# A hybrid decoder layer: zeros on TensorE at the start, 128 keys for the first query block, and a later place for the query lows

## What is computed

```python
h = h + 0.5 * swiglu(rmsnorm(h, ffn1_norm), ffn1_w_gate, ffn1_w_up, ffn1_w_down)   # 1024 -> 2816 -> 1024
proj = rmsnorm(h, mix_norm) @ w_in             # xp (512), q (16 heads of 64), k, v (2 heads), gates (2 x 1024)
branch_pool = causal_pool_mixer(xp, pool_w, pool_scale) @ w_pool_out
branch_attn = sliding_window_sink_attention(q, k, v, q_norm, k_norm, sinks) @ w_attn_out
h = h + (sigmoid(gate_pool) * branch_pool + sigmoid(gate_attn) * branch_attn) @ w_out
h = h + 0.5 * swiglu(rmsnorm(h, ffn2_norm), ffn2_w_gate, ffn2_w_up, ffn2_w_down)

# attention: nb = 4 blocks of 128 queries; each sees its own block of keys and the one before
kk = jnp.concatenate([jnp.pad(kb, pad)[:, :-1], kb], axis=2)      # block 0: 128 keys of zero padding
scores = einsum(qb, kk) * HEAD_DIM ** -0.5
band = (rel >= 0) & (rel < WINDOW)             # WINDOW = 128
in_seq = (nb > 0) | (kj >= 0)                  # block 0 sees none of the padding
scores = where(band & in_seq, scores, float32 min)
probs = softmax(concatenate([scores, sink]))[..., :-1]
out = einsum(probs, vv)
```

## Time and profile before

| | us |
|---|---|
| three runs of the kernel | 1060.41, 1062.83, 1062.62; median 1062.62 |
| the profiled execution, its own time | 1062.52 |
| its span, first to last instruction | 1060.7 |
| PE busy in it | 1044.2 |
| DVE, ACT, POOL busy | 663.9, 471.5, 433.6 |
| mean granted clock of PE | 0.998 |

### The profile page before, as it was taken

How to read it: one execution, slowest core, us unless ns; L and a number is a source line. 1 busy time by engine, 2 the same in 40 slices (tenths; PEclk the granted TensorE clock), 3 DMA queues, 4 the chain that set the end, 5 groups by cost and what they waited for, 6 DMA issues and landing times.

```text
span 1060.7 us, 15343 instructions
## 1 busy us (share of the span) xinstructions
PE 1044.2 (98%) x5952; PEld 907.8 (86%) x5952; DVE 663.9 (63%) x996; ACT 471.5 (44%) x814; POOL 433.6 (41%) x238
## 2 busy tenths in 40 slices
PE   7999999999999999999999999999999999999998
PEld 6878999998888888887777788888899999988887
DVE  6898777659340278426767657669997677584101
ACT  6443554455231334246667643333444555563120
POOL 1543423425444453345445445434423423354441
PEclk9999999999999999999999999999999999999999
DMA  5724757713323432221111122306367667333332
GB/s 194 226 81 122 186 152 182 204 62 119 100 99 93 146 112 80 88 89 60 60 60 59 60 61 99 99 27 201 99 159 181 188 168 188 104 100 99 99 99 99
DMA packets 42144, 124.76 MB, mean 118 GB/s; under 512 B 4320, under 2 KB 5344, under 8 KB 42080
## 3 DMA queue, kind: packets, MB, share of 16 engines
q1 hardware_dynamic: 37616, 107.89, 30.8%
q0 software_dynamic: 4320, 15.73, 8.6%
q10 hardware_dynamic: 144, 0.26, 0.1%
HBM read 121.76 MB, written 2.10 MB: 117 GB/s over the span
## 4 chain that ended last, share of the span: by engine, by line
PE 89%; DVE 7%; issue 1%; ACT 1%; DMA 1%; POOL 0%; DVEq 0%; SPq 0%; ACTq 0%
PE psum L524 18%; PE psum L526 18%; PE psum L525 18%; PE psum L619 10%; PE psum L620 9%; PE psum L621 9%; PE psum L854 1%; PE psum L869 1%; DVE u_blocks L1560 1%; PE psum L882 1%; PE psum L884 1%; PE psum L883 1%; DVE moving_sums_low L1585 1%; DMA up_s<-weights_dram 1%; PE psum L763 1%
## 5 line engine op out<-in xcount | busy, mean ns | idle before, releaser
L1394 POOL TENSOR_TENSOR w_low_in_place<-w_raw,w_high 128x1024 fp32r<-128x1024 f32 x68 | 169.6, 2497 | 212.3 <-ACT w_high L948 212.1
L948 ACT ACTIVATE w_high<-w_raw 128x1024 fp32r<-128x1024 f32 x118 | 124.5, 1055 | 212.9 <-DMA w_raw<-weights_dram 172.3
L1394 POOL TENSOR_TENSOR w_low<-w_raw,w_high 128x1024 fp32r<-128x1024 f32 x50 | 121.6, 2434 | 111.1 <-ACT w_high L948 111.1
L524 PE MATMUL psum<-hidden_high,w_high 128*128 128x512 f32 x352 | 137.0, 389 | 0.0
L525 PE MATMUL psum<-hidden_low,w_high 128*128 128x512 f32 x352 | 137.0, 389 | 0.0
L526 PE MATMUL psum<-hidden_high,w_low_in_place 128*128 128x512 f32 x352 | 136.9, 389 | 0.0
L1509 DVE SCALAR_TENSOR_TENSOR h<-psum,h 128x512 f32<-128x512 f32 x24 | 16.5, 689 | 151.0 <-PE psum L526 151.0
L524 PE MATMUL psum<-u_high,w_high 128*128 128x512 f32 x240 | 98.2, 409 | 0.0
L526 PE MATMUL psum<-u_high,w_low 128*128 128x512 f32 x240 | 93.9, 391 | 0.0
L525 PE MATMUL psum<-u_low,w_high 128*128 128x512 f32 x240 | 93.8, 391 | 0.0
L524 PE MATMUL psum<-ffn_u_high,w_high 128*128 128x512 f32 x222 | 88.6, 399 | 2.0 <-POOL w_low_in_place L1394 2.0
(11 more groups left out here) (259 smaller groups left out, 2849.6 us busy)
## 6 DMA issues: line engine op xcount, KB each, us to landing
w_raw<-weights_dram SPq DMA_DIRECT2D x118, 512.0 KB, 3.5
gate_a<-weights_dram SPq DMA_DIRECT2D x15, 512.0 KB, 6.1
gate_s<-weights_dram SPq DMA_DIRECT2D x15, 512.0 KB, 3.6
gate_s<-weights_dram POOLq DMA_DIRECT2D x15, 512.0 KB, 7.1
up_a<-weights_dram SPq DMA_DIRECT2D x15, 512.0 KB, 4.7
up_s<-weights_dram SPq DMA_DIRECT2D x15, 512.0 KB, 3.6
up_s<-weights_dram POOLq DMA_DIRECT2D x15, 512.0 KB, 8.3
gate_a<-weights_dram SPq DMA_DIRECT2D x15, 256.0 KB, 5.8
```

The lines of the kernel that those rows point to most:

```text
L524: pe.matmul(o, wh, xh, start=start, stop=False)
L948: act.activation(high[:, s, :], raw[:, s, :], ACT.Copy).then_inc(high_done, 1)
L1394: pool.tensor_tensor(wlow[:, s, :], raw[:, s, :], high[:, s, :], ALU.subtract).then_inc(low_done, 1)
```

## The change

Three parts.

1. **Zeros on PE at the start.** `first_tile` begins with `spin`: as soon as `sum_of_squares` is cleared, PE multiplies it with itself, five plain float32 products of 256 columns into a bank that is written afresh later. DVE waits for them (`spun`) before it adds the first square.

The diff, cut to its core:

```diff
@@
+        def is_first(nb):
+            return isinstance(nb, int) and nb == 0
+        def keys(nb):
+            return slice(BLK, 2 * BLK) if is_first(nb) else slice(0, 2 * BLK)
+        def halves(nb):
+            return (1,) if is_first(nb) else (0, 1)
+        def turned_count(nb, j):
+            return j if is_first(nb) else 8 * nb - 4 + 2 * j
@@ PE
+            def spin():
+                pe.wait_ge(summed[0], 1)
+                for i in range(5):
+                    mm = pe.matmul(psum[:, 0, 0:HT], acc[:, 0:P], acc[:, 0:HT], start=True, stop=True)
+                mm.then_inc(spun, 1)
@@ PE first_tile
+                spin()
                 pe.wait_ge(u_high[0], 1)
                 pe.wait_ge(quarter_high, 1)
@@ PE scores
-                            mm = pe.matmul(psum[:, 4 + kv, hh * 2 * BLK:(hh + 1) * 2 * BLK],
-                                           qs[r, 2 * j + hh, :], ks[r, :], start=(n == 0), stop=(n == 2))
+                            o = psum[:, 4 + kv, hh * 2 * BLK + keys(nb).start:(hh + 1) * 2 * BLK]
+                            mm = pe.matmul(o, qs[r, 2 * j + hh, :], ks[r, keys(nb)], start=(n == 0), stop=(n == 2))
@@ PE turn, weigh
-                for k in range(2):
+                for k in halves(nb):
...
-                pe.wait_ge(pt_low, 8 * nb + 2 * j + 2)
+                pe.wait_ge(pt_low, turned_count(nb, j) + len(halves(nb)))
@@ PE (and the same on ACT and DVE; POOL: all of block 0, then the loop from 1)
-            with pe.Fori(0, NB - 1) as nb:
+            for j in range(1, SLOTS):
+                step(0, j)
+            step(1, 0)
+            with pe.Fori(1, NB - 1) as nb:
@@ ACT exps
-                    act.activation(prob[:, j % 2, a, :], prob[:, j % 2, a, :], ACT.Exp,
+                    p = prob[:, j % 2, a, keys(nb)]
+                    act.activation(p, p, ACT.Exp,
@@ POOL normalize
-                p = prob[:, j % 2, :, :]
-                pool.tensor_tensor(p, p, rden[:, j % 2, :].unsqueeze(2).to_broadcast([P, 4, 2 * BLK]),
+                p = prob[:, j % 2, :, keys(nb)]
+                width = 2 * BLK - keys(nb).start
+                pool.tensor_tensor(p, p, rden[:, j % 2, :].unsqueeze(2).to_broadcast([P, 4, width]),
@@ DVE start
             second_half(1)
+            dve.wait_ge(spun, 1)
             for c in range(DT):
                 add_square(0, c, c)
@@ DVE
-            dve.memset(kn[:, 0:BLK], 0.0).then_inc(k_ready, 1)
-            dve.memset(vtok[:, 0, :], 0.0).then_inc(v_ready, 1)
@@ DVE maxima
-                dve.wait_ge(mask_set, nb + 1)
...
-                    dve.tensor_tensor_reduce(prob[:, b, a, :], psum[:, 4 + kv, hh * 2 * BLK:(hh + 1) * 2 * BLK],
-                                             mask[:, :], 1.0, 4 * MASKED, ALU.add, ALU.max,
+                    o = psum[:, 4 + kv, hh * 2 * BLK + keys(nb).start:(hh + 1) * 2 * BLK]
+                    dve.tensor_tensor_reduce(prob[:, b, a, keys(nb)], o,
+                                             consts[:, C_MASK + keys(nb).start:C_MASK + 2 * BLK],
+                                             1.0, 4 * MASKED, ALU.add, ALU.max,
@@ DVE step
-                    dve.tensor_copy(mask[:, :], consts[:, C_MASK:C_MASK + 2 * BLK]).then_inc(mask_set, 1)
                     block_factors(nb)
                 maxima(nb, j)
+                turned_part(*before)
+                if j in (1, 2):
+                    pool_gate(nb, j - 1)
                 if j == SLOTS - 1 and not (isinstance(nb, int) and nb == NB - 1):
                     stage(nb + 1)
-                if j in (1, 2):
-                    pool_gate(nb, j - 1)
-                turned_part(*before)
                 denominators(nb, j)
```

More of the change, by code:

```diff
@@ L1465, in _ @@
                 low_part(U_GATE + s, s)
-            step(0, 0)
-            with pool.Fori(0, NB - 1) as nb:
+            for j in range(SLOTS):
+                step(0, j)
+            step(1, 0)
+            with pool.Fori(1, NB - 1) as nb:
                 for j in range(1, SLOTS):
```

56 lines of the change are left out of this document (37 added, 19 removed).

## The result

| | before | after |
|---|---|---|
| time, median (range) | 1062.19 us (1060.41 to 1062.83) | 1050.67 us (1049.52 to 1052.04) |
| ratio to before, 95% interval | 1 | 0.9895 [0.9877, 0.9912] |
| profiled execution: time, span | 1062.52, 1060.7 | 1052.04, 1050.1 |

The change makes the kernel 1.05% faster, 11.5 us by the medians and 10.5 by the two profiled executions.

What follows compares the result with a forecast made beforehand. PE, busy 1044.2 of 1060.7 us, was taken to bound the kernel. From 1062.52, minus 1.6 (start), minus 6.3 (block 0), plus 2.4 (narrow scores), minus 2.3 (order) gave 1054.7 us, range 1051.1 to 1058.4.

Steps and rivals of the forecast that it cites:

- the price of the narrow scores: Block 0's score products on 128 columns: plain-f32 rate assumed, 0.22 us a pair, adding 2.4 us over four steps.
- cheap end: Block 0's narrow scores: a pair costs as one transpose of 128 columns, 0.11 us, changing the total by -0.2 us.
- Start, -1.6: Kernel start: zeros raise PE's clock early, the 25th product starts at 12.44, and 1.6 us are saved.
- The bounds of -0.3 and -2.6 for single runs: Kernel start: the gain from zeros varies between these values in single runs, as the moment of the clock's rise differs.
- Block 0, -6.3 without the scores' price: Attention, block 0 on 128 keys: four steps fall from 37.43 to 31.1 us, 1.9 of it waits.
- Order, -2.3: Attention, query lows behind probability lows: steps 3 of blocks 1 and 2 save 1.4 us, steps 1 save 0.9.
- The fall of the clock, kept: First FFN, 72.7 to 76.1 us: PE's clock still falls, costing some 1.6 us; its going only widens the range.
- (a): Block 0's scores: narrow score products are cheap, giving 1052.1 us; chance 0.32.
- (b): Block 0: other engines hold steps at 8.89 us, so only the waits go, giving 1056.7 us; chance 0.08.
- (e): Block 0's scores: a narrow pair costs 0.87 us instead of 0.15, making the kernel slower at 1069.3 us; chance 0.04.
- (c): Start: zeros don't count as work for the clock, or the DVE chain eats the gain, 1056.3 us; chance 0.07.
- (d): Block changes: query lows come late under POOL's low part, adding 4.2 us at three changes, 1058.9 us; chance 0.04.

Runs made afterwards that it cites:

- e4: Changed kernel with block 0's scores taken over 256 columns again instead of 128; 1051.6 us.
- e11: Changed kernel with block 0's scores taken over only the last 64 of its 128 keys; 1050.4 us.
- e2: Kernel before with only block 0 cut to its own 128 keys, no zeros and the old VectorE order; 1054.75 us, ratio 0.9928.
- e16: One more profile of the e2 kernel, unchanged and without zeros; 1052.93 us.
- e5: Changed kernel with VectorE's copy of the next block's key factors split and taken out of the head of step 0; 1049.61 us, ratio 0.9879.
- e1: Kernel before with only the five products of zeros at the start and VectorE's wait for them; 1060.32 us, ratio 0.9978.
- e3: Kernel before with only VectorE's order changed: probability lows first, then pool gate, then next block's query lows; 1060.76 us, ratio 0.9979.

## Why the prediction was wrong

**The failed step is the price of the narrow scores**, "So I take the dear end: +2.4". This term of the sum was mis-sized, and its mechanism was wrong. It is not +2.4 but -0.6: four times the 0.15 us between e4 and the changed kernel. The argument was that the two narrow kinds in the trace ran at 0.85 ns a column, as plain float32 does, and the fast rate was shown for wide products only. But the transposes' 0.11 us for 128 columns is not a rate a column; e11 shows 0.11 for 64 columns too. So the price of a narrow pair has a floor that doesn't follow its columns. The transposes and the narrow scores have in common that 128 columns of new weights are loaded each time, and that load is the likely floor. The row for the right answer was in hand, the transposes as the "cheap end", and that rival had 0.32.

The rest, term by term (profile against profile):

- **Start, -1.6:** measured -1.54, of which 0.36 came only in the first FFN. The 25th product is at 12.88, not at 12.44, because PE waited 0.89 us for a low part of x. The sum product was to be at 26.2, counted from the 27.82 at which the chain of the earlier trace rows has it; the chain of the changed kernel has it at 26.64 (the timeline has 27.66 and 26.48). That zeros count as work for the clock was right. Over many profiles the gain at the sum product is 1.1 us; without zeros the full pace began anywhere from 9.2 (e2) to 11.9 us (e16), so a single profile of before says little about it. The bounds of -0.3 and -2.6 for single runs have no working; against the mean with zeros, 26.19, the eight starts without lie 0.5 to 1.8 us later.
- **Block 0, -6.3 without the scores' price:** -6.3 and -0.6 are -6.9, measured -6.93. The undisturbed step was to be 7.77, less 0.15 is 7.62, as measured. The waits went as foreseen, with POOL's low part in step (0, 1) ending at 484.03, 4.7 us behind the step's start, where 4.9 was worked out.
- **Order, -2.3:** measured -1.59. The steps 3 of blocks 1 and 2 gained their 0.7 each (9.58 to 8.86, 9.60 to 8.86), but 0.4 of it came back in each of the steps (2, 0) and (3, 0). The prediction asked what is late next and looked at the query lows and at the denominators. What was late was the copy at the head of DVE's step 0, now under POOL's low part. e5 removes it and brings 1.1 us.
- **The fall of the clock, kept, with its going in the range:** this is the second term that failed. It was kept in the profiled execution alone (granted clock 0.998), and went in the other three (1.000); over all kernels it stands in 50 of 60 executions without zeros and in 6 of 33 with five. The prediction saw that the shift might change it, and kept it without a row that speaks for either. The median lies 1.4 us below the profiled time from which all terms were counted. The range's low end was rival (a) less 1.0, while the form with the short blocks and without the fall is worth 2.5 (a first FFN of 347.16 us in place of 349.66), so it didn't reach.

From the forecast: 1054.7 - 3.0 (scores) + 0.7 (order) + 0.1 (start) - 0.5 (the stretch behind the attention, which scatters) = 1052.0, the profiled 1052.04; and 1.4 less is the median. The chances don't add as written: the parts named for faster come to nearly 0.94, not 0.90.

Of the rivals, (a), cheap scores with 1052.1, is the one that came true. That its number meets the profiled 1052.04 is luck: the scores brought 0.4 more than it had, the order 0.7 less, and the stretch behind the attention scattered by 0.5. (b), steps held at 8.89 by other engines, and (e), narrow scores at 0.87 a pair, are refuted by the steps of 7.6. (c) is refuted by e1, whose pace, sum product and ratio all show the gain. (d), the query lows late under POOL's work, didn't happen: PE's waits in the steps (2, 0) and (3, 0) of the changed kernel are for probability lows, and no step (nb, 0) of e5 shows a wait. But its mechanism did, on an instruction that wasn't thought of. The Trainium skill ("SBUF — State Buffer", section "Who interferes with whom") names copies too among the DVE operations that can take the pair of ports shared with GpSimd; 1.64 and 1.52 us for copies in e3 and in the changed kernel, against 0.16 before and 0.17 in e5, agree.

## What to carry to other kernels

A product can have a floor that its columns don't show: where each one loads new weights, read the distance of the weight loads beside narrow products before pricing another one. When an instruction is moved out of a wait, look at everything that the earlier step start now meets on a second engine, small copies included. And where two engines exclude each other, one race early in the kernel can go with two populations of executions; compare terms within one of them. Read the granted clock of every execution and not of the profiled one alone, since an edit can change how often the clock falls elsewhere.

## What was unexpected

- Products of zeros, 128 x 128 by 256 columns of plain float32, raise TensorE's clock: with five of them the real products stand 0.23 us apart from 6.2 to 7.3 us on (nine profiles), with two, and 2.4 us of idleness behind, only from 11.9 (one profile), and without any from 9.2 to 11.9 (eight).
- With the five zeros, the fall of the clock in the first FFN is rare: 6 of 33 executions against 50 of 60 without.
- A product of 64 rows by 64, 128 or 256 columns costs 0.11, 0.11 or 0.12 us a pair, two rows' halves side by side.
- A DVE copy of 128 x 16 elements took 1.52 us beside GpSimd's 2.39, and eight DVE products of 128 x 512 with two operands in SBUF 9.5 or 11.15 us, by which engine began first.
